# A gated delta rule on 64-token chunks instead of 128, and earlier transfers for the first modulation

## What is computed

```python
mod = silu(c) @ ada_w[i] + ada_b[i]            # ada_w[i]: 1024 x 6144
h = rmsnorm(x, norm_g[i, 0]) * (1 + sc1) + sh1
```

```python
decay = exp(where(i >= s, g_cum[i] - g_cum[s], -inf))      # 64 x 64 per chunk
a_low = where(i > s, (k_beta @ k.T) * decay, 0)
u, w  = solve(eye + a_low, [v * beta, k_beta * exp(g_cum)])
attn  = (q @ k.T) * decay
for each chunk:                                            # state: 128 x 128
    v_new = u - w @ state
    o     = (q * exp(g_cum)) @ state + attn @ v_new
    state = state * exp(g_last) + (k * exp(g_last - g_cum)).T @ v_new
```

## Time and profile before

| | before |
|---|---|
| median of 3 runs | 3384.2 us (3379.8 to 3389.3) |
| the profiled execution, its own time | 3382.1 us |
| its span in the profile | 3380.3 us |
| PE busy | 2991 us (88 %) |
| DVE busy | 1635 us (48 %) |
| ACT busy | 1158 us (34 %) |
| POOL busy | 202 us (6 %) |
| mean granted clock of PE | 0.947 |

### The profile page before, as it was taken

One profiled execution on the slowest core, in us unless ns is written; L12 is line 12 of the kernel. 1 busy time (PEld: TensorE's weight loads), 2 busy tenths in 40 slices (PEclk: granted clock), 3 DMA queues, 4 the chain that ended last, 5 costly groups with the idle time before them and its releaser, 6 DMA issues.

```text
span 3380.3 us, 45348 instructions
## 1 busy us (share of the span) xinstructions
PE 2991.3 (88%) x20206; PEld 2436.6 (72%) x20206; DVE 1634.8 (48%) x2186; ACT 1157.5 (34%) x1506; POOL 201.9 (6%) x155
## 2 busy tenths in 40 slices
PE   3999999698999879999578888789999897799999
PEld 2887888476888768887366666567888785478887
DVE  5666553553677643232556565544333456443332
ACT  2225233342223134152443334323222456532221
POOL 1010000101222110001100000000000100010000
PEclk9999999899999989999789888899999998999999
DMA  6454543120000032222101001012232220022321
GB/s 226 183 196 149 199 175 114 50 87 34 3 3 3 3 125 100 100 97 90 50 25 38 26 25 38 13 38 77 81 115 82 96 76 24 1 100 84 110 87 68
DMA packets 41571, 269.70 MB, mean 80 GB/s; under 512 B 4256, under 2 KB 4512, under 8 KB 13344
## 3 DMA queue, kind: packets, MB, share of 16 engines
q1 hardware_dynamic: 38976, 260.01, 21.7%
q10 hardware_dynamic: 2400, 6.78, 0.5%
HBM read 264.68 MB, written 2.10 MB: 79 GB/s over the span
## 4 chain that ended last, share of the span: by engine, by line
PE 77%; DVE 12%; ACT 8%; issue 1%; DMA 1%; POOL 1%; POOLq 0%; DVEq 0%; SPq 0%; ACTq 0%
PE ps L599 19%; PE ps L606 19%; PE ps L601 19%; PE ps L1934 2%; PE ps L2570 1%; PE ps L1566 1%; PE ps L944 1%; PE ps L1549 1%; PE ps L956 1%; PE ps L1560 1%; PE ps L962 1%; DVE WL L413 1%; POOL ACC L500 1%; DVE k L988 1%; PE ps L463 1%
## 5 line engine op out<-in xcount | busy, mean ns | idle before, releaser
L599 PE MATMUL ps<-HH,WH 128*128 128x512 f32 x1928 | 767.3, 398 | 57.6 <-ACT HH L575 41.0
L601 PE MATMUL ps<-HH,WL 128*128 128x512 f32 x1928 | 758.4, 393 | 0.0
L606 PE MATMUL ps<-HL,WH 128*128 128x512 f32 x1928 | 735.4, 393 | 2.4 <-DVE HL L556 1.7
L413 DVE TENSOR_TENSOR WL<-ST,WH 128x2048 fp32r<-128x2048 f32 (+2 forms) x259 | 470.9, 1820 | 285.3 <-ACT WH L405 285.2
L405 ACT ACTIVATE WH<-ST 128x2048 fp32r<-128x2048 f32 (+2 forms) x211 | 382.7, 1814 | 320.2 <-PE ps L606 300.1
L599 PEld LDWEIGHTS ps<-HH,WH 128*128 128x128 f32 x1928 | 367.3, 191 | 146.9 <-issue 69.2
L606 PEld LDWEIGHTS ps<-HL,WH 128*128 128x128 f32 x1928 | 366.2, 190 | 83.2 <-DVE HL L556 4.5
L601 PEld LDWEIGHTS ps<-HH,WL 128*128 128x128 f32 x1928 | 367.5, 191 | 78.6 <-issue 2.9
L599 PE MATMUL ps<-GH,WH 128*128 128x512 f32 x928 | 361.6, 390 | 0.0
L601 PE MATMUL ps<-GH,WL 128*128 128x512 f32 x928 | 361.0, 389 | 0.0
L606 PE MATMUL ps<-GL,WH 128*128 128x512 f32 x928 | 359.8, 389 | 0.0
(11 more groups left out here) (350 smaller groups left out, 4052.4 us busy)
## 6 DMA issues: line engine op xcount, KB each, us to landing
ST<-w_m SPq DMA_DIRECT2D x64, 1024.0 KB, 4.8
ST<-w_gu SPq DMA_DIRECT2D x44, 1024.0 KB, 4.8
ST<-w_ada SPq DMA_DIRECT2D x40, 1024.0 KB, 5.7
ST<-w_dn SPq DMA_DIRECT2D x32, 704.0 KB, 4.0
ST<-w_gin SPq DMA_DIRECT2D x16, 1024.0 KB, 4.9
ST<-w_cin SPq DMA_DIRECT2D x12, 1024.0 KB, 4.8
ST<-w_rkv SPq DMA_DIRECT2D x12, 1024.0 KB, 5.0
ST<-w_kv SPq DMA_DIRECT2D x8, 1024.0 KB, 4.8
```

The lines of the kernel that those rows point to most:

```text
L413: o = e.tensor_tensor(WL[:, j % 3, cut], ST[:, pos % 3, cut], WH[:, j % 3, cut].bitcast(F32), ALU.subtract)
L599: e.matmul(big.tile((tag, m))[:, :], wh[:, k, c0:c0 + P], H[:, k, :], start=(k == 0), stop=False)
L601: e.matmul(big.tile((tag, m))[:, :], wl[:, k, c0:c0 + P], H[:, k, :], start=False, stop=False)
L606: o = e.matmul(big.tile((tag, m))[:, :], wh[:, k, c0:c0 + P], L[:, k, :], start=False, stop=(k == kt - 1))
```

## The change

The delta rule is rebuilt on 64-token chunks. A head has eight chunks; two neighbours lie in the lower and upper half of the partitions. All products within a chunk are 64x64 or have one side of 64 (`rows(p)`), the inverse has levels 1 to 5, the recurrence eight steps. Decay, beta and the norms of q, k and o are no longer applied as full tiles: they are columns with one value per token, applied as a scalar per partition and chunk (`along`). Sums of squares of q and k are products with a single column of ones, and the norm of o is a reduction on DVE and an Ln/Exp on 4 columns. o is formed with tokens on partitions and transposed at the end. POOL masks. Steps are 21 (front), 20 (back) and 32 (project), merged by relative place, as in the RWKV scan. The splits of the next weight tiles come in halves. The projection has two PSUM banks instead of three, the rest six instead of five. The products of a projection come in the order high x high, low x high, high x low. The split for the output projection moves into the last loop.

In the opening W0's eight quarters are sent ahead of everything that can wait: 0 and 1 on SP ahead of the first weight tile, 2, 3 and 5 on ACT behind x and the tables, 4, 6 and 7 on SP. DVE does the eight sums first, the last of them in four pieces, then the norm and the first weight's split; gain and scaled tiles are done in two halves of four.

```diff
@@ vector_conv
-            vector_rms(e, "conv")
-            vector_low(e, 0)
             e.wait_ge(*norm_act.at("silu"))
-            for k in range(8):
+            for k in range(7):
...
-            vector_columns(e, "begin")
-            vector_gain(e, "conv", 0, 0, 1, 8)
-            e.wait_ge(*norm_vec.at("conv", "gain"))
-            vector_split(e, "conv", lambda k: SM[:, 8 + k:9 + k], lambda k: modcol(0, 0, k))
+            e.wait_ge(s_ad[7], 16)
+            e.wait_ge(*ada.at("begin", 6))
+            for b in flush["first half"] + flush["second half"]:
+                bs = slice(512 * b, 512 * b + 512)
+                e.scalar_tensor_tensor(out=S0[:, bs], in0=W0[:, 7, bs], scalar=SM[:, 7:8], in1=S0[:, bs],
+                                       op0=ALU.mult, op1=ALU.add).then_inc(*ada.up("begin", 7, b))
+            vector_rms(e, "conv")
+            vector_low(e, 0)
+            for n, half_ in enumerate(("first half", "second half")):
+                vector_columns(e, half_)
...
+                vector_split(e, "conv", lambda k: SM[:, 8 + k:9 + k], lambda k: modcol(0, 0, k), None, range(KT)[ks])
@@ gdn_order
+            out = [("project", 0)] * GDN_PROJECT
             for h in range(9):
...
+                steps = []
+                if h:
+                    steps += [((i + 0.5) / GDN_BACK, 0, "head", h - 1) for i in range(GDN_BACK)]
+                if h < 7:
+                    steps += [((i + 0.5) / GDN_PROJECT, 1, "project", h + 1) for i in range(GDN_PROJECT)]
+                if h < 8:
+                    steps += [((i + 0.5) / GDN_FRONT, 2, "head", h) for i in range(GDN_FRONT)]
+                    steps += [((i + 0.9) / 6, 3, "low", (h, i)) for i in range(6)]
+                else:
+                    steps += [((i + 0.7) / 8, 3, "split", i) for i in range(7)]
+                out += [(kind, n) for _, _, kind, n in sorted(steps)]
@@ tensor_head: sums of squares and products of k
+            for r, sq in enumerate((SQ, SK)):
                 e.wait_ge(*gdn_act.at("square", h, r))
-                e.wait_ge(*gdn_b.free(("norm", h, r)))
-                e.matmul(gdn_b.tile(("norm", h, r))[:, :], tb("ones"), n1, start=True,
-                         stop=True).then_inc(*gdn_mm.up("norm", h, r))
+                for c2 in range(4):
+                    o = e.matmul(gdn_b.tile(("sums", h))[:, 4 * r + c2:4 * r + c2 + 1], sq[:, P * c2:P * c2 + P],
+                                 tb("ones")[:, 0:1], start=True, stop=True)
...
+            for c2, p in PAIRS:
+                cs = slice(P * c2 + 64 * p, P * c2 + 64 * p + 64)
+                o = e.matmul(gdn_b.tile(("gram", h))[rows(p), P * c2:P * c2 + P], QK[:, 1, cs], QK[:, :, cs],
+                             start=True, stop=True)
@@ tensor_head: inverse
+            for lev in range(1, GDN_LEVELS):
...
+                for c2, p in PAIRS:
+                    o = e.matmul(ps[rows(p), 64 * c2:64 * c2 + 64], AL[rows(p), c2, 64:128], TN[rows(p), c2, :],
+                                 start=True, stop=True)
+                o.then_inc(*gdn_mm.up("u", h, lev))
@@ tensor_head: recurrence
+            for c in range(8):
+                c2, p = c // 2, c % 2
+                cs = slice(64 * c, 64 * c + 64)
                 if c:
...
+                    e.matmul(gdn_b.tile(("ws", h, c))[rows(p), 0:P], WT[:, cs], SG[:, :], start=True,
                              stop=True).then_inc(*gdn_mm.up("ws", h, c))
+                o = e.matmul(po1[rows(p), P * c2:P * c2 + P], QK[:, 0, cs], SG[:, :], start=True, stop=True)
...
+                    e.matmul(gdn_b.tile(("s", h, c))[:, 0:P], KD[rows(p), c2, :], XV[rows(p), c2, :], start=True,
                              stop=True).then_inc(*gdn_mm.up("s", h, c))
+                o = e.matmul(po2[rows(p), P * c2:P * c2 + P], AL[rows(p), c2, 0:64], XV[rows(p), c2, :], start=True,
+                             stop=True)
@@ vector_head: end of a head (ACT: square, Ln, Exp, Square on 4 columns between)
+            e.tensor_tensor(v4(OT[:, :]), v4(gdn_b.tile(("o1", h))[:, :]), along(GEG[:, :, h], P),
+                            ALU.mult).then_inc(*gdn_vec.up("o1", h))
...
+            e.tensor_tensor(OT[:, :], OT[:, :], gdn_b.tile(("o2", h))[:, :], ALU.add).then_inc(*gdn_vec.up("o2", h))
+            yield
+            e.wait_ge(*gdn_act.at("osq", h))
+            e.tensor_reduce(f, v4(WT[:, :]), mybir.AxisListType.X, ALU.add).then_inc(*gdn_vec.up("osum", h))
...
+            newton(e, f, f2, qs, "o", h)
+            e.wait_ge(*gdn_vec.at("o", h, "rstd"))
+            e.tensor_tensor(v4(OT[:, :]), v4(OT[:, :]), along(f, P), ALU.mult).then_inc(*gdn_vec.up("scaled", h))
@@ vector_gdn
-            for c in range(4):
-                cs = slice(P * c, P * c + P)
-                o = e.tensor_tensor_scan(GG[0:8, cs], tb("ones")[0:8, :], t[0:8, cs], 0.0, ALU.mult, ALU.add)
+            for c in range(8):
+                cs = slice(64 * c, 64 * c + 64)
+                o = e.tensor_tensor_scan(GG[0:8, cs], tb("ones")[0:8, 0:64], t[0:8, cs], 0.0, ALU.mult, ALU.add)
@@ scalar_program, sync_program
+            for k in (2, 3, 5):
+                load_first(e, k)
             scalar_conv(e)
...
             e.dma_start(CC[:, :], cols).then_inc(s_cols, 16)
+            for k in (0, 1):
+                load_first(e, k)
...
                 if pos == 0:
-                    for k in range(1, 8, 2):
-                        e.dma_start(W0[:, k, :].rearrange("p (b f) -> p b f", b=4),
-                                    first_ada(k)).then_inc(s_ad[k], 16)
+                    for k in (4, 6, 7):
+                        load_first(e, k)
```

More of the change, by code:

```diff
@@ L655, in plan_conv @@
             plan_rms("conv")
-            flush["begin"] = [2, 3, 0, 1]
-            for b in flush["begin"]:
+            flush["first half"], flush["second half"] = [2, 0], [3, 1]
+            for b in flush["first half"] + flush["second half"]:
                 sml.use(("mod", b), mod, b)
@@ L680, in tensor_conv @@
             tensor_rms(e, "conv")
-            tensor_columns(e, "begin")
+            tensor_columns(e, "first half")
+            tensor_columns(e, "second half")
             tensor_dense(e, "conv_in", HH, HL, split_high("conv"), split_low("conv"))
@@ L1815, in gdn_order @@
         def gdn_order():
-            HEAD, PROJECT, HALF = 37, 32, 21
-            out = [("project", 0)] * PROJECT
-            taken = {("project", 0): PROJECT}
-            def step(kind, h, n):
-                if 0 <= h < 8 and taken.get((kind, h), 0) < n:
-                    out.append((kind, h))
-                    taken[kind, h] = taken.get((kind, h), 0) + 1
-                    return True
-                return False
-            for h in range(9):
-                for i in range(HALF):
-                    step("head", h - 1, HEAD)
-                    step("project", h + 1, PROJECT)
-                    step("head", h, HEAD)
-                    step("project", h + 1, PROJECT)
-                    out.append(("low", (h, i)))
-                while step("head", h - 1, HEAD) or step("project", h + 1, PROJECT):
-                    pass
@@ L1839, in build @@
+            return out + [("split", 7)]
         GDN = gdn_order()
@@ L1856, in plan_project @@
                 plan_upto(("take", j), j + 2)
-                due.extend((number[sched[pos]], part) for pos in take["take", j] for part in range(4))
+                due.extend((number[sched[pos]], part) for pos in take["take", j] for part in range(2))
                 for r in (2 * n, 2 * n + 1):
@@ L1916, in plan_gdn @@
             big.use(("ab", 0), gdn_vec, "u")
-            tmp.use(("dt",), gdn_vec, "sums")
-            sml.use(("gc",), gdn_vec, "rows")
-            in_turn(GDN, {"project": plan_project, "head": plan_head, "low": plan_low})
+            tmp.use(("dt",), gdn_vec, "decay cum")
+            sml.use(("gc",), gdn_vec, "columns")
+            sml.use(("betas",), gdn_vec, "betas")
+            in_turn(GDN, {"project": plan_project, "head": plan_head, "low": plan_low, "split": no_steps})
             plan_settle("gdn", len(due))
@@ new lines, in tensor_head @@
+            for c2 in range(4):
+                cs = slice(P * c2, P * c2 + P)
+                o = e.transpose(gdn_b.tile(("kt", h))[:, cs], QK[:, 1, cs], tb("ident"))
+            o.then_inc(*gdn_mm.up("kt", h))
+            yield
+            ps = gdn_b.tile(("t0", h))
+            e.wait_ge(*gdn_b.free(("t0", h)))
+            e.wait_ge(*gdn_pool.at("t0", h))
+            for c2, p in PAIRS:
+                o = e.matmul(ps[rows(p), 64 * c2:64 * c2 + 64], TTh[rows(p), c2, :], tb("idk", rows(p)), start=True,
+                             stop=True)
@@ new lines, in tensor_head @@
+            e.wait_ge(*gdn_vec.at("tt", h, GDN_LEVELS - 1))
+            e.wait_ge(*gdn_vec.at("xv", h))
+            e.wait_ge(*gdn_b.free(("us", h)))
+            for c2, p in PAIRS:
```

(20 more changed lines are left out.)

732 lines of the change are left out of this document (344 added, 388 removed).

## The result

| | before | after |
|---|---|---|
| median | 3383.3 us | 3243.4 us (3239.6 to 3249.9, 4 runs) |
| the profiled execution, its own time | 3382.1 us | 3245.5 us |
| its span | 3380.3 us | 3243.7 us |
| PE busy | 2991 us | 2960 us |
| DVE busy | 1635 us | 1564 us |

The ratio is 0.9587, with a 95 % interval of 0.9568 to 0.9605: 140 us less, where 118 were forecast. PE does 31 us less of busy time (time at the lower clock counts as busy), and its span is 137 us shorter, so 106 of them are time in which it stood.

The account below looks back on a forecast made before the run. PE was taken to pace the delta rule loops, losing time to waits and clock; transfers, then DVE, the opening. Opening -13.2, setup +1.5, loops and ends -105, output -1: -118 us, to 3264 profiled, 3265 median (3208 to 3348).

Parts of the forecast that it names:

- setup, up to the first fourth tile: Delta rule setup: eight short scans for four, 24 small transposes and products for four, +1.5 us (0 to 3).
- two signs of being wrong: Delta rule: inverse's DVE steps not shorter than 0.5 us, or PE waiting in every chunk of the recurrence.
- part 3: PE's work in a full loop: 42.6 us of products plus 9.5 for shape changes, 52.1, about as before.
- The unknown of the sum: Products of k with k and q, eight of 128x64, no measured row: 0.9 to 1.8 us, 1.4 taken.
- rival B: Loops: shape changes cost nothing behind fp32r products, a loop 48 to 50 us, total 3212; chance 0.17.
- The other rule that the prediction weighed: Inverse: row tiles can't share a PSUM bank at once, so groups take twice as long, 7 us more a loop.
- part 4: Full loop's waits and clock: 3.5 us of waits, 1.9 for the clock, loop 57.5 us (50 to 71).
- one named chain: Head's end: adds, square, reduction, small norm and scaling, about 5 us, stop PE for 2 us.
- Rival C: Loops stay bound by handovers between engines, 71 us each, gain only at ends and opening, 3346; chance 0.26.
- rival D: Lower clock throughout the loops from short products broken by drains, 95 us a loop, total 3490; chance 0.07.
- part 1: Opening: modulation weights sent ahead and summed first, first scaled tile at 44.6 against 57.8, 13.2 us less (9 to 15).
- part 5: First loop 44 us (-7), loops 1 to 6 -80, after last projection 46 plus 30 (-18), output projection -1.

Follow-up runs that it names:

- twos: Kernel after with the delta rule's projection steps taken two at a time, 16 projection runs a loop instead of 26: 3234.6 us, ratio 0.9558.
- in turns: Kernel after with its delta rule steps alternating one by one between heads and projection, as in the kernel before: 3276.0 us, ratio 0.9682.
- the run with idle products: Kernel after with paired projection steps, z later, earlier table load, plus an unread identity product per head step behind the last projection: 3240.5 us, ratio 0.9581.
- fours: Kernel after with the delta rule's projection steps taken four at a time, 8 projection runs a loop: 3271.2 us, ratio 0.9656.

## Why the prediction was right, and by which steps

| step | forecast | measured |
|---|---|---|
| first scaled tile | 44.6 (-13.2) | 43.2 (-14.6) |
| setup, up to the first fourth tile | +1.5 | +1.3 |
| first loop | 44 | 42.2 |
| a full loop | 57.5 | 55.0 |
| loop 7, to L1983 of the last head | 46 | 46.3 |
| back part of head 7 | 30 | 28.4 |
| output projection and all behind it | -1 | +0.3 |
| profiled execution | 3264 | 3245.5 |

The mechanism was the forecast one in the opening and the loops: PE has as much to do as before, and its pauses go. Of the 18.5 us that the sum was too long, 15 lie in the six full loops. The two signs of being wrong that it named did not come: the inverse's steps on DVE take 0.42, and in the loops PE does not wait in every chunk of the recurrence (in the tail, with nothing else left to do, the chain of a chunk sets the pace). DVE is busy 33 us a loop (35 forecast), ACT 17 (18).

**PE's work (part 3).** Products as priced. Timeline of PE in a loop at the full clock:

```profile
1758.04 1.09 PE L1983 MATMUL ps<-v,t 64*64 64x128 f32 x16
1759.06 1.11 PE L1989 MATMUL ps<-t,e 64*128 64x64 f32 x16
1760.10 0.50 PE L1860 MATMUL ps<-HH,WH 128*128 128x512 f32 x1
1760.43 0.39 PE L1860 MATMUL ps<-HH,WL 128*128 128x512 f32 x1
1760.66 0.40 PE L1860 MATMUL ps<-HL,WH 128*128 128x512 f32 x1
1760.99 0.43 PE L2007 MATMUL ps<-s,qk 128*64 128x128 f32 x2
```

The last product of a group is followed 0.33 later where the shape changes, 0.23 where it doesn't, and so is the first behind a change: 0.1 on each side of this run. The small group ahead of a change loses as well: the eight products of L1983 take 1.02 to the next start, where eight of their shape took 0.87 in the scan. So a run costs 0.2 to 0.3; twos measured 0.2. The group of L1989, the state's factors, takes 1.04, where 0.6 (0.5 to 0.9) and its share of the changes were taken: this term was too small. The unknown of the sum, products of 128 rows and 64 columns, and the sums of squares ahead of them:

```profile
1773.41 0.94 PE L1918 MATMUL ps<-TB,e 128*128 128x1 f32 x8
...
1775.18 1.09 PE L1925 MATMUL ps<-qk 128*64 128x128 f32 x16
1776.21 0.50 PE L1860 MATMUL ps<-HH,WH 128*128 128x512 f32 x1
```

Eight of them take 1.03 with the change behind them, so they run side by side: the lower bound of 0.9 to 1.8, where 1.4 was taken. The sums of squares take 1.77, from 1773.41 to 1775.18 (1.8 forecast). In all a loop at clock 1.00 is 54.0 less 1.1 of waits, 52.9 of work, against 52.1. So rival B is out: with changes for nothing, 42.6 of work and 1.1 of waits would make 43.7, not 54.0. The other rule that the prediction weighed falls too: in "TensorEngine Tiling (Array Packing)" of the Trainium skill, Restrictions and Gotchas, different row tiles can't be in one PSUM bank at a time, but eight 64x64x64 products of after in one bank (L1967, two instructions each) take 0.51 from their start to that of the next group (2065.44 to 2065.95, in loop 7), where 0.47 was forecast for pairs side by side.

**Waits and clock (part 4), the term that was mis-sized.** The prediction took 3.5 us of waits and 1.9 for the clock a loop; it is 1.1 and 1.0 (six loops: 324 at 54.0, and 6 of dips). A loop was forecast 2.5 us too long: 2.4 by the waits and 0.9 by the clock, less 0.8 by which the work was taken too small. Its one named chain, the end of a head, is the one that is left, at 0.9 where 2 was taken. The other 1.5 had no row of their own, only the scan's 5 % as a comparison. That the relative places put projection products between the inverse's steps fits this: with the same form in turns the waits are 3.9 a loop. Turned round: before, a loop lost 11 us by waits and 7 by the clock (0.10 of 70.9), which leaves 52.7 of work, about that of after. After, it loses 2 in all. Rival C is out by the waits, rival D by the clock of 0.98.

**The argument for the gain.** The prediction built on the two longest waits being the norm's. The run without the norm bears it out: 100 us. It also shows that the waits were only half of what the norm cost. The prediction put no price on the clock before the change; its sum, which counts the loop after from its parts, didn't need one.

**The opening (part 1).** DVE waits 4.1 us for the data of its second sum and then hardly at all: 14.6, near the end of 15 given for that. The three DMA issues ahead of ACT's work took 6.3 us of its queue (1.66 to 8.00) and were hidden, as said.

**The ends (part 5), in part luck.** They hold to 1.8 us each (first loop 42.2, loop 7 46.3, back part 28.4). But the clock has a mean of 0.69 in loop 7 and 0.50 behind it, of which the prediction said nothing; 0.31 of loop 7's 46.3 us are up to 14 us lost by the clock. That the counts hold in spite of it is luck: something else in them was too long. For the chunk this can be read: 2.40, with 2.3 forecast for the upper level, where the chain is 1.83 by the rows of the run with idle products. The forecast had started from a chunk of before (1.99, at clock 1.00), with other products, and added 0.3 for three changes of shape. (And 7 x 2.3 is 16.1, not the 16.4 that it gives.) For loop 7 it stays open which part was too long.

## What to carry to other kernels

A full-width chain between two products can cost more than its wait: without it TensorE's clock was higher too, and here that doubled the price (5.6 us of waits and 5.4 by the clock a head). So scale by columns with one value per token, and put the steps of independent parts by their relative place, so that dense products lie evenly between dependent ones. Form and order remove the same waits: of the 125 us that both give beside the opening, the form without the order gets 93 and the order without the form 47. Fewer changes of shape pay only as long as no new pause opens: twos won some 9 us, fours lost 23.

## What the runs showed of the hardware that was not expected

- The lower clock level can be granted for 6 us and more while PE is busy throughout, behind a pause of 1.7 us (fours, 1818.7 to 1824.8; 26 us of waits in all six loops, clock 0.90). Two stretches at the lower level came in the six loops of after too, one of them (1829 to 1839) with PE busy in full for the 18 us ahead of it (from 1811 on); what releases it isn't shown. The sum of the waits doesn't tell the clock: 26 us in six loops went with 0.90, 33 with 0.97 (before without the norm) and 55 with 0.94 (old form, new order).
- 128x128 fp32 products of no use, two a chunk, went with a granted clock of 1.00 in a recurrence that ran at 0.50 without them, and the chunk got 0.21 us shorter in spite of them.
- A change of array shape costs about 0.1 us on each side of a run of fp32r 128x512 products (0.33 from start to start where 0.23 is usual), seen beside groups of 64x128 and of 128x64.
- Eight fp32 products on 128 rows by 64 columns of the array, in pairs for the two halves of the output, take 1.03 us with the change behind them; a 128x128 one takes 0.22, so that one by one they would take 1.8. They run side by side.
